# Moving the last tile's norm turn ahead of four weight splits at the end of the second MLP, in a two-block network on one Trainium2 core

## The reference

```
h = post_norm_residual(h, sq_relu_mlp(modulate(h, sh2, sc2), mlp_w1[1], mlp_w2[1]), g2, ln_g[1, 1], ln_b[1, 1])
...
h = concatenate([meta, h], axis=1)          # 16 meta tokens go ahead of the 1024
u = _rmsnorm(h, mix_norm_g)
p = u @ w_in_2                              # 14 groups of 128 columns
p_pool, p_bval, p_bgate, p_cgate, p_cx = split(p)
```

## Time and profile before

| | us |
|---|---|
| median of 3 runs (lowest, highest) | 3675.88 (3674.2, 3679.75) |
| the profiled execution, its own time | 3675.58 |
| its span, first to last instruction | 3673.8 |
| PE busy | 3331.4 (91%) |
| DVE busy | 1901.2 (52%) |
| ACT busy | 1181.0 (32%) |
| POOL busy | 475.1 (13%) |

### The profile page before, as it was taken

One profiled execution on the slowest core, in us unless ns is written; L12 is line 12 of the kernel. 1 busy time (PEld: TensorE's weight loads), 2 busy tenths in 40 slices (PEclk: granted clock), 3 DMA queues, 4 the chain that ended last, 5 costly groups with the idle time before them and its releaser, 6 DMA issues.

```text
span 3673.8 us, 37805 instructions
## 1 busy us (share of the span) xinstructions
PE 3331.4 (91%) x15463; PEld 2774.8 (76%) x15463; DVE 1901.2 (52%) x2630; ACT 1181.0 (32%) x1725; POOL 475.1 (13%) x291
## 2 busy tenths in 40 slices
PE   3999887879999999688799999997996799999997
PEld 2888776668888888576678888886884678888886
DVE  6624677565555554844644434446686643333334
ACT  5311686252222121431522222224445341122222
POOL 4001464120000000400300000003380000000000
PEclk9999999989999999898899999998997999999998
DMA  6435220202333331002011111111120111111111
GB/s 192 138 115 171 74 61 24 98 18 92 93 102 93 96 99 57 32 7 63 29 57 48 48 51 46 52 47 29 30 76 30 52 46 46 46 47 56 59 47 46
DMA packets 191335, 239.53 MB, mean 65 GB/s; under 512 B 9719, under 2 KB 149482, under 8 KB 191162
## 3 DMA queue, kind: packets, MB, share of 16 engines
q1 hardware_dynamic: 180538, 199.45, 17.7%
q0 software_dynamic: 9184, 32.41, 2.4%
q10 hardware_dynamic: 1440, 5.24, 0.4%
HBM read 220.24 MB, written 16.83 MB: 65 GB/s over the span
## 4 chain that ended last, share of the span: by engine, by line
PE 75%; DVE 14%; ACT 8%; issue 3%; DMA 1%; POOL 0%; SPq 0%; DVEq 0%; ACTq 0%; POOLq 0%
PE psum L515 24%; PE psum L516 24%; PE psum L517 24%; DVE small L639 2%; ACT temp L822 2%; ACT U_hi L521 2%; DVE small L1281 1%; DVE H L1386 1%; DVE PT_lo L526 1%; ACT prob L1247 1%; DVE small L664 1%; DVE U_lo L526 1%; DVE split L526 1%; PE psum L585 1%; ACT split L521 1%
## 5 line engine op out<-in xcount | busy, mean ns | idle before, releaser
L515 PE MATMUL psum<-U_hi,split 128*128 128x512 f32 x2108 | 836.6, 397 | 61.8 <-DVE split L526 37.5
L516 PE MATMUL psum<-U_lo,split 128*128 128x512 f32 x2108 | 830.5, 394 | 0.0
L517 PE MATMUL psum<-U_hi,split 128*128 128x512 f32 x2108 | 829.3, 393 | 0.0
L521 ACT CAST split<-raw 128x1024 fp32r<-128x1024 f32 x261 | 268.0, 1046 | 1260.9 <-PE psum L517 883.0
L515 PE MATMUL psum<-split,A_hi 128*128 128x512 f32 x1536 | 598.9, 390 | 2.9 <-ACT temp L822 2.9
L517 PE MATMUL psum<-split,A_lo 128*128 128x512 f32 x1536 | 598.1, 389 | 0.0
L516 PE MATMUL psum<-split,A_hi 128*128 128x512 f32 x1536 | 598.0, 389 | 0.0
L1386 DVE TENSOR_TENSOR H<-H,psum 128x512 f32<-128x512 f32 x416 | 281.3, 686 | 585.2 <-PE psum L517 585.2
L515 PEld LDWEIGHTS psum<-U_hi,split 128*128 128x128 f32 x2108 | 402.0, 191 | 154.1 <-DVE split L526 38.8
L526 DVE TENSOR_TENSOR split<-raw,split 128x1024 fp32r<-128x1024 f32 x261 | 326.3, 1265 | 286.7 <-ACT split L521 283.7
L517 PEld LDWEIGHTS psum<-U_hi,split 128*128 128x128 f32 x2108 | 401.9, 191 | 85.2
(11 more groups left out here) (307 smaller groups left out, 3940.1 us busy)
## 6 DMA issues: line engine op xcount, KB each, us to landing
raw<-in_mlp_w_dram SPq DMA_DIRECT2D x128, 512.0 KB, 4.3
raw<-in_ada_w_dram SPq DMA_DIRECT2D x96, 512.0 KB, 4.3
raw<-in_w_in_dram SPq DMA_DIRECT2D x38, 512.0 KB, 3.9
raw<-in_w_up_dram SPq DMA_DIRECT2D x32, 512.0 KB, 4.0
raw<-in_w_down_dram SPq DMA_DIRECT2D x32, 512.0 KB, 4.2
H<-in_x_dram ACTq DMA_DIRECT2D x8, 512.0 KB, 4.5
raw<-d_q SPq DMA_DIRECT2D x32, 128.0 KB, 2.7
raw<-d_k SPq DMA_DIRECT2D x16, 256.0 KB, 3.9
```

The lines of the kernel that those rows point to most:

```text
L515: pe.matmul(out, l_hi, r_hi, start=start, stop=False)
L516: pe.matmul(out, l_hi, r_lo, start=False, stop=False)
L517: return pe.matmul(out, l_lo, r_hi, start=False, stop=stop)
L521: return act.copy(hi, src).then_inc(*k.hi.inc(*key))
```

## The change

The two calls that run `mlp1` on ACT and on DVE get the argument `tile_first=True`. PE's, POOL's and SP's programs are the same.

```diff
@@ scalar_program @@
-    act_mlp(k, act, on, "mlp1", BOUNDARY[2], (1, 1), lambda tt: act_boundary(k, act, on, BOUNDARY[3], tt))
+    act_mlp(k, act, on, "mlp1", BOUNDARY[2], (1, 1), lambda tt: act_boundary(k, act, on, BOUNDARY[3], tt), True)
@@ vector_program @@
-    dve_mlp(k, dve, on, "mlp1", BOUNDARY[2], (1, 1), ALPHA, lambda tt: dve_boundary(k, dve, on, BOUNDARY[3], tt))
+    dve_mlp(k, dve, on, "mlp1", BOUNDARY[2], (1, 1), ALPHA, lambda tt: dve_boundary(k, dve, on, BOUNDARY[3], tt), True)
```

## The result

| | before | after |
|---|---|---|
| median of 19 runs each (lowest, highest), us | 3675.88 (3674.2, 3680.41) | 3683.87 (3680.64, 3687.35) |
| the profiled execution, its own time / span, us | 3675.58 / 3673.8 | 3683.12 / 3681.2 |
| mean granted clock | 0.959 | 0.955 |

The ratio is 1.0018, with a 95% interval of 1.0011 to 1.0024: 6.6 us slower, between 4.0 and 8.8 us. The medians lie 8.0 us apart. Forecast were 6.4 us.

A forecast was written before the change was run, and what follows sets the result against it. PE bounds the kernel, busy 91% of the span, with tile 7's chain on the path during its rest. A 6.2 us delay at the meta tokens plus 0.2 made 6.4 us on 3675.58: 3682.0, median 3682.3, range 3678 to 3687.

The forecast's parts named there:

- The chain: Tile 7's chain on DVE and ACT at the end of `mlp1`: starts 7.6 us earlier, 12.4 us to its last hat.
- The weights: Casts and low parts behind tile 7's last hat: casts from 2549.75, PE starts at 2552.15 after standing still for 14 us.
- The products: PE's (1, 0) and (2, 0), 48 matmuls after an idle PE: 13.2 us, range 12.38 to 13.84, done at 2565.3.
- The meta tokens: From DVE's product of (2, 0) to PE's first meta transpose: 4.2 us unchanged, so everything from there comes 6.2 us later.
- Hidden work: Unit 4's load, cast and low part, sigmoids and tables: covered by PE's 48 matmuls until 2565.3, costed at nothing.
- Behind it: PE's meta and chunk 1 transposes at low clock as before, costed at nothing; then 0.2 us, the delay passed on.
- The 0.2 us for slow matmuls beside chunk 1: PE's (3, 0) and (0, 1) beside the taking of chunk 1: matmuls staying slow cost 0 to 1.1 us, taken as 0.2.
- The delay is passed on whole: From (3, 0) on PE does not rest until 2751 and other engines follow its products, so the delay reaches the end.
- the clock works against it twice: Rival: 48 matmuls take 13.84 us, later matmuls also slow; 7.95 us and up to 2 more, 3684 to 3686; chance 0.34.
- the long end of the 48: PE's (1, 0) and (2, 0) taking 13.84 us, the longest of four earlier stretches of 48 matmuls after an idle PE.
- 0.48, 0.13 and 0.02: Chances of the forecast loss of 5.4 to 7.3 us, of less being lost (3679.0), and of no difference (3675.9).
- The faster rival: Rival: PE has unit 1 by 2546.0, so hat, sigmoids and meta tokens come 7.6 us sooner, 3668.3 us; chance 0.03.

The follow-up runs named there:

- mirror: Kernel before, with the meta tokens' measure, root and hat moved ahead of the sigmoids and the product of (2, 0): 3675.75 us, ratio 0.9999.
- two-unit kernel: Changed kernel, but units 1 and 2 split ahead of tile 7's turn, only units 3 and 4 behind it: 3672.73 us, ratio 0.9988.
- delayed kernel: Kernel before, with nine extra DVE measures (5.6 us) ahead of the meta tokens' own measure: 3682.86 us, ratio 1.0014.

## Why the prediction was right

The time lies in the range, and the sign and the mechanism at the place of the change were forecast; the ratio gives 6.6 us where the sum gave 6.4. Step by step:

- *The chain.* Forecast: it starts where the additions end, 7.6 us earlier, with its length unchanged. Measured: 1.31 us after the start of the additions; from its start to the start of the last hat 12.37 us, as before.
- *The weights.* Forecast: casts 1.15 us after the last hat's start, PE 2.40 us behind them, from the same order at `post0`. Measured 1.15 and 2.41. PE's rest is 12.64 us where I said 14, since (0, 0) ended 1.4 us later in this execution; its end is what counts.
- *The products.* Forecast 13.2 us for 48 matmuls. Measured 12.40 and 12.79 in the two profiles, inside the bounds of the earlier trace rows. This term was 0.4 to 0.8 us too large; it is the only one of the sum up to the meta transposes that was off.
- *The meta tokens.* Forecast 4.2 us from DVE's product to the transposes. Measured 2566.81 - 2562.63 = 4.18.
- *Hidden work.* The fourth cast was done over 7 us ahead of DVE's product, with the sigmoid of (0, 0) behind it. Right.
- *Behind it.* Local loss at the meta transposes: 5.35 and 5.69 us (34.39 after the additions in the second profile), against 6.2. From there to (3, 0) no change was forecast; 8.12 us before became 8.47 and 6.91. The 0.2 us for slow matmuls beside chunk 1 did not appear: the first 10.62 us from (3, 0) ran at a clock of 1.00 in both kernels. "The delay is passed on whole": this step was wrong. The stage from (3, 0) takes 1.6 and 3.3 us more in the two profiles, by slow stretches behind short matmuls. I had seen the granted clock of the stage, 0.97, and priced its change only within the rival, as "up to 2 more of such luck".

The errors go against each other. Counted from the additions, as means of the two profiles of each kernel, the change costs 5.6 us at the meta transposes (28.70 and 28.54 became 34.05 and 34.39), gives 0.3 back up to (3, 0) and costs 2.5 more up to L2036: 7.8 us, near the 8.0 of the medians, where the sum said 6.2 + 0.2; the ratio says 6.6. That the sum came as near as it did is in part luck. The rival "the clock works against it twice" was right about the later slow stretches, which cost more than its "up to 2" in one of the two profiles, and wrong about the long end of the 48 and about slow matmuls beside chunk 1. In the chances, 0.48, 0.13 and 0.02 make 0.63 and not 0.61. The faster rival was decided as stated: unit 1 came at 2550.0 (2552.2 on the scale of before), not before 2546.0. That it was the lateness of two units, and nothing else in the new order, is shown by splitting these two first: then a chain that starts 3.46 us after the additions instead of 8.90 is a gain. That the chain had been on the path before is shown by the mirror's and the two-unit kernel's meta transposes, which both moved; that this alone buys time is not, since the mirror's 4.1 us were not found again at its end.

## What to carry to other kernels

Before work is moved ahead of a queue, look up when its consumer wants each thing that now stands behind it; here two of four units were wanted within 8 us and two were not, and cutting the list there turned a loss of some 7 us into a gain of 4. Where the same order stands elsewhere in the kernel, its rows price the waits at the new place to a tenth of a microsecond; the matmuls that start slow behind a rest they priced only to 0.8 us. A gain or loss of a few microseconds at one place may be changed again by the clock further on, so judge such an edit at its own place in the trace and by the spread of many runs, not by one.

## What was not expected

PE's clock falls to half in stretches of about 3 us inside a stretch of 168 us in which PE never rests, at the end of groups of 24 matmuls of 128x16 or a few wide matmuls behind them; with 3 in place of 24 no such stretch remained in the projection. Each stretch costs about 1.65 us, and their number in the stage was 3 in both profiles of before, 4 and 5 in those of the change, 5 in the delayed kernel. That a delay of 5.4 us changes their number, and that a gain of 4.1 us can vanish in them, fits the medians, but with one or two profiles for each kernel it is argued, not shown, and the 3 of a kernel that begins the stage late and the 4 of one that begins it early speak against a plain rule; nor is it settled what sets their number. Behind L2036 the profiles that keep the short matmuls fall in two groups that no experiment here explains: the rest of the span takes 917.8 to 918.8 us, or 920.8 to 921.1. The first profile of the change is in the second group and its second profile in the first.
